# Expert weights of a mixture layer in 1 MB quarters, with the first gate matrix loaded in the stage before

## The reference, cut to what matters

```python
g_idx  = argmax(t @ w_rg + b_rg)                  # one of 4 groups for each token
ids, w = top-2 of the 8 experts of that group     # so 512 (token, expert) pairs over 32 experts
y_e    = (silu(h @ w_gate[e]) * (h @ w_up[e])) @ w_down[e]   # 2048 -> 512 -> 2048
x      = x + gate * sum_e combine[:, e] * y_e
out    = modulated RMS norm of x
```

## Time and profile before

| what | value |
|---|---|
| median of 3 runs | 2301.48 us (2300.1 to 2301.67) |
| the profiled execution's own time | 2300.72 us |
| its span, from first to last instruction | 2299.0 us |
| mean granted TensorE clock | 0.990 |
| TensorE matmul busy | 2142.7 us, 93% |
| VectorE busy | 1379.7 us, 60% |
| ScalarE busy | 731.1 us, 32% |
| moved by DMA | 760.64 MB, mean 331 GB/s |

### The profile page before, as it was taken

One profiled execution on the slowest core, in us unless ns is written; L12 is line 12 of the kernel. 1 busy time (PEld: TensorE's weight loads), 2 busy tenths in 40 slices (PEclk: granted clock), 3 DMA queues, 4 the chain that ended last, 5 costly groups with the idle time before them and its releaser, 6 DMA issues. The chain is left out here.

```text
span 2299.0 us, 35407 instructions
## 1 busy us (share of the span) xinstructions
PE 2142.7 (93%) x14337; PEld 1621.8 (71%) x14337; DVE 1379.7 (60%) x2163; ACT 731.1 (32%) x1324; POOL 40.9 (2%) x62
## 2 busy tenths in 40 slices
PE   7999999999999999899999979998898888898886
PEld 6899999888999998788898755554444444444443
DVE  6888889988888899755556453333333333333334
ACT  6444554554445554556555320000000000000001
POOL 0010000000000000020000000000000000000000
PEclk9999999999999999999999989999999999999998
DMA  8898777988887779654344189999999999999996
GB/s 336 339 341 324 281 266 282 351 341 334 331 326 279 268 278 370 239 207 161 137 147 151 51 355 429 431 430 429 429 432 430 432 430 429 429 432 429 432 428 288
DMA packets 72496, 760.64 MB, mean 331 GB/s; under 512 B 8224, under 2 KB 11200, under 8 KB 13888
## 3 DMA queue, kind: packets, MB, share of 16 engines
q1 hardware_dynamic: 72240, 758.31, 82.3%
q10 hardware_dynamic: 144, 0.79, 0.1%
HBM read 756.12 MB, written 2.95 MB: 330 GB/s over the span
## 5 line engine op out<-in xcount | busy, mean ns | idle before, releaser
L1230 DVE TENSOR_TENSOR s_w_tail<-s_raw,s_w_head 128x1024 fp32r<-128x1024 f32 x292 | 345.7, 1226 | 19.1 <-ACT s_w_head L832 19.0
L1020 PE MATMUL b_ps<-s_h_head,s_w_head 128*128 128x256 f32 x1184 | 340.9, 288 | 0.0
L832 ACT ACTIVATE s_w_head<-s_raw 128x1024 fp32r<-128x1024 f32 x292 | 294.4, 1052 | 141.1 <-DMA s_raw<-in_w 87.7
L1021 PE MATMUL b_ps<-s_h_tail,s_w_head 128*128 128x256 f32 x1184 | 334.8, 283 | 0.0
L1022 PE MATMUL b_ps<-s_h_head,s_w_tail 128*128 128x256 f32 x1184 | 334.8, 283 | 0.0
L1345 DVE CUSTOM_DVE_ANT_0 s_raw<-s_raw,s_c_row 128x2048 f32<-128x2048 f32 x128 | 292.6, 2286 | 0.2
L2464 PE MATMUL b_ps<-s_raw,s_window 128*64 128x256 f32 x2048 | 227.6, 380 | 38.7 <-DMA s_raw<-in_w_up 20.7
L2464 PEld LDWEIGHTS b_ps<-s_raw,s_window 128*64 128x64 f32 x2048 | 155.2, 137 | 116.3 <-issue 30.6
L1020 PEld LDWEIGHTS b_ps<-s_h_head,s_w_head 128*128 128x128 f32 x1184 | 226.7, 192 | 4.2 <-issue 3.9
L1021 PEld LDWEIGHTS b_ps<-s_h_tail,s_w_head 128*128 128x128 f32 x1184 | 227.0, 192 | 0.3
L1022 PEld LDWEIGHTS b_ps<-s_h_head,s_w_tail 128*128 128x128 f32 x1184 | 226.8, 192 | 0.0
(11 more groups left out here) (356 smaller groups left out, 3429.5 us busy)
## 6 DMA issues: line engine op xcount, KB each, us to landing
s_raw<-in_w SPq DMA_DIRECT2D x198, 1024.0 KB, 5.1
s_raw<-in_w_ada SPq DMA_DIRECT2D x128, 1024.0 KB, 6.2
s_raw<-in_w_gate SPq DMA_DIRECT2D x16, 4096.0 KB, 32.8
s_raw<-in_w_up SPq DMA_DIRECT2D x16, 4096.0 KB, 30.7
s_raw<-in_w_down SPq DMA_DIRECT2D x32, 2048.0 KB, 26.9
s_down<-in_w_down SPq DMA_DIRECT2D x16, 2048.0 KB, 27.2
s_spare<-in_w_gate SPq DMA_DIRECT2D x8, 4096.0 KB, 32.9
s_down<-in_w_gate SPq DMA_DIRECT2D x8, 4096.0 KB, 32.9
```

The source lines that it names most:

```text
L832: act.activation(w_head[:, g % SPLITS, cols], raw[:, ring, cols], ACT.Copy)\
L1020: pe.matmul(out, head, m_head, start=first, stop=False, skip_group_check=True)
L1021: pe.matmul(out, head, m_tail, start=False, stop=False, skip_group_check=True)
L1230: dve.tensor_tensor(w_tail[:, g % SPLITS, cols], raw[:, slot["w", g], cols], w_head[:, g % SPLITS, cols].bitcast(F32), ALU.subtract)\
```

## The change

- The ring keeps its four slots of 4 MB, but every matrix is loaded as four quarters of 1 MB (8 KB for a partition out of rows of 32 KB), each with an arrival semaphore of its own (`arrived[slot][q]`) and a release of its own: `used` goes up 12 times for an expert instead of 4, and SP waits for one quarter's release before it loads that quarter.
- Slot 0 (`first_slot`) is allocated ahead of the second attention, whose ka, kb, v, s_buf, p_t, squares and one of the two q buffers now lie in it. SP loads the gate of expert 0 into it at the end of the second attention's list, after the last weight piece and after `onorm B`. `experts` then loads only up and down of expert 0 at its start.
- `x_head` and `x_tail` become one buffer `x_parts`, in four quarters by width, which lie over the four quarters of slot 3; quarter q of expert 1's gate is loaded when 4(q + 1) tiles are gathered.
- `window` is copied in two halves; the first half of the first window is copied in the middle of the gather, and TensorE starts expert 0 with it.
- Semaphores of the first block are used again in the second attention, with counts that run on. The router logits are put in `o_rstd` instead of q.

```diff
+        full(sp, ("onorm", "B"))
+        for q in range(QUARTERS):
+            sp.dma_start(first_slot[:, q, :], d["w_gate"][0, :, q * CHUNK_ELEMS:(q + 1) * CHUNK_ELEMS])\
+              .then_inc(first_arrived[q], 16)
...
-        x_head, x_tail = (passing.enter_context(nc.sbuf_tensor(f"s3_{name}", [P, TT, D], F32R))
-                          for name in ("x_head", "x_tail"))
+        x_parts = passing.enter_context(nc.sbuf_tensor("s3_x_parts", [P, QUARTERS, 2, TT, 512], F32R))
...
+    def load_quarter(sp, e, c, q, slot):
+        src = (w_gate, w_up, w_down)[c][pick_e, :, q * CHUNK_ELEMS:(q + 1) * CHUNK_ELEMS]
+        sp.dma_start(ring[slot][:, q, :], src.rearrange("a p n -> (a p) n")).then_inc(arrived[slot][q], 16)
+    def arrival(eng, seq, q, turns_before=0):
+        eng.wait_ge(arrived[seq % SLOTS_E][q], turns_before * 16 + (seq // SLOTS_E * 16 + 16))
...
-        for c in range(PIECES_E):
-            load_expert_piece(sp, 0, c)
+        for c in (1, 2):
+            for q in range(QUARTERS):
+                load_quarter(sp, 0, c, q, c)
...
-            sp.wait_ge(sem["gathered"], KT)
             for c in range(PIECES_E):
-                if c:
-                    sp.wait_ge(sem["used"], min(c, 2))
-                load_expert_piece(sp, 1, c, 1)
+                for q in range(QUARTERS):
+                    seq = PIECES_E + c
+                    if c == 0:
+                        sp.wait_ge(sem["gathered"], KT // QUARTERS * (q + 1))
+                    else:
+                        sp.wait_ge(sem["used"], QUARTERS * (seq - SLOTS_E) + q + 1)
+                    load_quarter(sp, 1, c, q, seq % SLOTS_E)
...
                     for c in range(8):
-                        if c % 4 == 0:
-                            pe.wait_ge(arrived[(3 * j + c // 4) % 4], ...)
+                        if c in (0, 2):
+                            pe.wait_ge(sem["window"], of(2, 1 + c // 2))
+                        arrival(pe, PIECES_E * j + c // 4, c % 4, four * PIECES_E)
                         ...
-                        if c % 4 == 3:
-                            ins.then_inc(sem["used"], 1)
+                        ins.then_inc(sem["used"], 1)
...
                     for m_ in range(FT):
-                        if m_ == 0: ...
-                        elif m_ == 2: ...
+                        arrival(pe, PIECES_E * j + 2, m_, four * PIECES_E)
                         ...
-                        if m_ % 2:
-                            ins.then_inc(sem["used"], 1)
+                        ins.then_inc(sem["used"], 1)
...
+            if m == 9:
+                dve.wait_ge(sem["read_a"], 4)
+                dve.wait_ge(sem["read_v"], 4)
+                dve.tensor_copy(window[:, 0:8, :], picked[:, 0:8, 0:WINDOW]).then_inc(sem["window"], 1)
...
-        dve.tensor_copy(window[:, :, :], picked[:, :, 0:WINDOW]).then_inc(sem["window"], 1)
+        dve.tensor_copy(window[:, 8:KT, :], picked[:, 8:KT, 0:WINDOW]).then_inc(sem["window"], 1)
```

More of the change, by code:

```diff
@@ L58, with __init__ @@
 class Tally:
-    def __init__(self):
+    def __init__(self, before=None):
         self.order = {}
+        self.before = before or {}
     def add(self, sem, event, it=0):
@@ L67, in add @@
         assert (event, it) not in table, (sem, event, it)
-        table[event, it] = len(table) + 1
+        table[event, it] = self.before.get(sem, 0) + len(table) + 1
     def at(self, sem, event, it=0, each=1):
@@ L1485, in _ @@
             x_done(dve, DEPTH - 1)
+    passed_on = [f"full{b}" for b in range(8)] + [f"raw{n}" for n in range(RAW)]
+    return {name: sem[name] for name in passed_on}, {name: len(tally.order[name]) for name in passed_on}
 HEADS_2 = 16
@@ L2208, with experts @@
 SLOTS = PICKED + WINDOW
[L2209 removed]
+PIECES_E = 3
+USED_E = PIECES_E * QUARTERS
 TAIL_AT = {1: 1, 3: 2, 7: 3}
 PART_BANKS = ((0, 1, 2, 3), (6, 7, 4, 5))
[L2216 removed]
+def experts(nc, whole, ctx, d, x, ssq_x, c0, mod, mod_dram, out, shared, first_slot, arrived):
     sem_names = ["consts", "squared", "rstd", "affine", "read_a", "read_v", "dense_row", "dense_h", "exp_in", "exp", "pairs", "sums", "sums_read", "starts", "x_head", "x_tail", "picks",
                  "gathered", "window", "used", "gate_exp", "hidden", "turned", "hidden_t", "y_half",
[L2230 removed]
+                 "weights_t", "y_scaled", "part", "x_added", "out_ready", "stored", "rows", "dense_gate", "dve_chain", "pool_chain"]
     sem = {n: whole.enter_context(nc.semaphore(f"b3_{n}")) for n in sem_names}
[L2232 to L2233 removed]
     def sb(name, shape, dt=F32):
         return ctx.enter_context(nc.sbuf_tensor(f"s3_{name}", shape, dt))
[L2238 to L2240 removed]
+    second_slot = sb("second_slot", [P, QUARTERS, CHUNK_ELEMS])
+    third_slot = sb("third_slot", [P, QUARTERS, CHUNK_ELEMS])
     picked = sb("picked", [P, KT, SLOTS])
@@ L2343, in _ @@
                     for c in range(PIECES_E):
-                        sp.wait_ge(sem["used"], four * (4 * PIECES_E) + (PIECES_E * (j + 1) + min(c, 2)))
-                        load_expert_piece(sp, four * 4 + (j + 2), c, j + 2)
+                        for q in range(QUARTERS):
+                            seq = PIECES_E * (j + 2) + c
+                            sp.wait_ge(sem["used"], four * (4 * USED_E) + (QUARTERS * (seq - SLOTS_E) + q + 1))
+                            load_quarter(sp, four * 4 + (j + 2), c, q, seq % SLOTS_E)
             for e in (EXPERTS - 2, EXPERTS - 1):
                 for c in range(PIECES_E):
-                    sp.wait_ge(sem["used"], PIECES_E * (e - 1) + min(c, 2))
-                    load_expert_piece(sp, e, c, e)
-            sp.wait_ge(sem["used"], PIECES_E * (EXPERTS - 1))
+                    for q in range(QUARTERS):
+                        seq = PIECES_E * e + c
+                        sp.wait_ge(sem["used"], QUARTERS * (seq - SLOTS_E) + q + 1)
+                        load_quarter(sp, e, c, q, seq % SLOTS_E)
+            sp.wait_ge(sem["used"], USED_E * (EXPERTS - 1))
         for n, row in ((2, mod_dram[7:8, :]), (1, mod_dram[6:7, :])):
@@ L2519, in _ @@
                 for c in range(PIECES_E):
-                    pe.wait_ge(arrived[c] if c < 3 else second_half[0], e * 16 + 16)
+                    for q in range(QUARTERS):
+                        arrival(pe, c, q, e)
                 for side in range(2):
@@ L2684, in _ @@
                 loop.link(dve.tensor_tensor(hid, psum[:, 0, 0:T], hid, ALU.mult))
-                dve.wait_ge(sem["used"], e * PIECES_E + 2)
+                dve.wait_ge(sem["used"], e * USED_E + 2 * QUARTERS)
                 dve.tensor_tensor(hidden[:, 1, :], psum[:, 1, 0:T], hid, ALU.mult).then_inc(sem["hidden"], 1)
                 start = dve.value_load(starts_i[0:1, bass.ds(e + 1, 1)], min_val=0, max_val=PICKED)
-                dve.tensor_copy(window[:, :, :], picked[:, :, bass.ds(start, WINDOW)]).then_inc(sem["window"], 1)
+                for ks in (slice(0, 8), slice(8, KT)):
+                    dve.tensor_copy(window[:, ks, :], picked[:, ks, bass.ds(start, WINDOW)]).then_inc(sem["window"], 1)
                 for b in range(2):
@@ L2810, in build @@
                                       ("gain3", [P, KT]), ("sconst", [P, 36]))}
+        first_slot = ctx.enter_context(nc.sbuf_tensor("first_slot", [P, QUARTERS, CHUNK_ELEMS], F32))
+        arrived = [[ctx.enter_context(nc.semaphore(f"b3_arrived{slot}_{q}")) for q in range(QUARTERS)]
+                   for slot in range(SLOTS_E)]
         with ExitStack() as part:
-            second_attention(nc, ctx, part, d, x, ssq_all, c0, mod, mod_dram, shared)
+            second_attention(nc, ctx, part, d, x, ssq_all, c0, mod, mod_dram, shared, first_slot, arrived[0],
+                             ring_sems, ring_counts)
         with ExitStack() as part:
-            experts(nc, ctx, part, d, x, ssq_x, c0, mod, mod_dram, out, shared)
+            experts(nc, ctx, part, d, x, ssq_x, c0, mod, mod_dram, out, shared, first_slot, arrived)
```

94 lines of the change are left out of this document (42 added, 52 removed).

## The result

The changed kernel took 2309.54 us (median of 5, 2308.65 to 2311.17) against 2301.48 for the kernel before: ratio 1.0037, 95% interval 1.0025 to 1.0049. The forecast was 2308.9 us, slower. The profiled execution was the slowest of the five, 2311.17 us against 2300.72 before. A second set of runs of the same kernel gave 2311.24 us, 1.0042 (1.0028 to 1.0056).

The account below looks back on a forecast made before the run. The prediction took the expert stage's unbroken weight stream as the bound: last landing +11.4 us at 420.5 GB/s, prefetch included, less 4.0 at the end, gave +7.4, so 2308.9 us median; range 2295 to 2317.

Parts of the forecast that it names:

- What bounds: Expert stage: one unbroken stream of weight transfers at 430 GB/s is the bound, not TensorE.
- The prefetch: Start of the expert stage: early gate of expert 0 and early slot 3 quarters save 3 quarters, 7 us of stream.
- The size of a transfer: Expert stream: 8 KB rows in 1 MB transfers run at 420.5 GB/s instead of 430; last landing +11.4 us.
- The second way: Expert stream: rate from 32 and 16 KB rows (432, 426 GB/s); a cost in each row doubles again, giving 414.5.
- The tail: After the last landing: TensorE takes quarters as they land, done 1.77 us (1.9 with a wait) later, not 5.9; −4.0 us.
- The sum: Later last landing plus shorter end: +11.4 − 4.0 = +7.4 us, 2308.1 profiled, 2308.9 median.
- the signs of being wrong: Expert stage: rate 424 or more, DMA share under 0.98 after 1365 us, or TensorE's clock falling for over two short stretches.
- The fresh rate: Rival on the expert stream: 8 KB rows hold 424 to 427 GB/s; 2295.0 us at 427; chance 0.25.
- size costs nothing: Rival on the expert stream: rate stays at 430 GB/s, giving 2288.6 us; chance 0.07.
- the cost is in each row, or each transfer: Rival on the expert stream: 414.5 GB/s, 2322.3 us (417 gives 2316.7); chance 0.12 together with the late-slot rival.
- The start is not what I think: Rival at the stage's start: slot 3 or 0 frees late, stream breaks, 2 to 5 us lost; within a shared 0.12.

Follow-up runs that it names:

- mixed: The changed kernel with only experts 0 to 3 and 31 in quarters and the 27 between in 4 MB matrices; 2295.29 us, 0.9971.
- mixed_32: The changed kernel with only experts 0 to 2, 30 and 31 in quarters, the others in 4 MB matrices; 2292.71 us, 0.9959.
- parts_32: The kernel before the change, each transfer issued as four of every fourth partition, rows kept at 32 and 16 KB; 2303.52 us, 1.0007.
- no_prefetch: The changed kernel with expert 0's gate loaded at the start of the expert stage, not in the second attention; 2318.42 us, 1.0073.
- apart_8k: The changed kernel, each matrix in two 2 MB transfers of alternate quarters (8 KB rows), arrival and release by full matrix; 2320.28 us, 1.0079.
- halves: The changed kernel with 2 MB pieces (16 KB rows) instead of quarters for load, arrival and release; 2298.02 us, 0.9983.
- whole_arrival: The changed kernel, but TensorE waits for all four quarters of a matrix at the first; loads and releases unchanged; 2314.84 us, 1.0058.
- whole: The changed kernel with 4 MB matrices (32 KB rows) instead of quarters for load, arrival and release; 2300.76 us, 0.9995.

## Why the prediction was right, step by step

**What bounds.** Right: the stream. The DMA share is 1.01 from 1363 to 2262 us, and wherever a run changed rows, landings or prefetch, the last landing moved with the stream. In mixed and mixed_32, as in before and parts_32, TensorE then ends the layer on its own work, without a wait for the last matrix.

**The prefetch.** Right. The early quarters went out at 1274.94 (1274.5 forecast); TensorE began expert 0 at 1362.13, 31.1 us after the stage's first issue (31.6 forecast). Undoing the early gate costs 8.5 us of the stage; I had 7 for gate and slot 3 together, against the kernel before, and 9 for this run. What I had not seen is that the gate alone gives this. no_prefetch keeps the early quarters of slot 3 and the early window, and its stage is 965.9 − 949.0 = 16.9 us longer than before; the rate costs 21.3 and the tail gives back 3.9, so these two are worth about 0.5 us, an estimate.

**The size of a transfer.** The term that decided was taken as 420.5 GB/s and measured as 420 to 421. The number was right, and in part by luck. I chose it because the stream would be like the stretch at 903 to 919 us "in size and in depth", and the depth is not the cause: the queue is now 27.3 us deep instead of 8.3 and the rate is the same,

```profile
s_third_slot<-in_w_up SPq DMA_DIRECT2D x32, 1024.0 KB, 27.3
```

The 427 GB/s of the earlier trace rows are not from 8 KB rows alone: from 97 to 107 us, 0.73 of the 4.27 MB went over a second queue.

```profile
q10 hardware_dynamic: 135, 0.73, 17.5%
```

A later stretch is SP's queue alone, with rows of 8 KB, and still over 421; this stays unexplained.

```profile
123.00:132.00 9.00, 9.00 (x64) 8.41 (x63) 6.08 (x7) 4.52 (x6) 0.00 (x0) 1.00 1.01 425
```

The second way, a cost that sits in each row, is the mechanism that parts_32 and apart_8k show. I had it only as a bound and among the rivals, at 414.5 GB/s with a small chance. It was too low, because 426 GB/s, read from 8 us, is 428 in a long stretch (halves). With 428 the same working gives 420.2, which is the measured rate.

In a queued stream no fixed cost of microseconds is paid for each transfer in line: parts_32 has four times the transfers of before at 429 GB/s, and after lands 1 MB every 2.49 us. The Trainium skill gives a fixed cost of about 2.0 us for each transfer ("DMA: Bandwidth & Descriptors", section Anatomy of one DMA — SWDGE (gpsimd) path), measured on transfers issued from GpSimd, while these are issued from SP. The prediction tied this cost to the 341 GB/s of the page's section Bandwidth, which does not state it as their cause; no run here measures a transfer by itself.

**The tail.** Right: 1.94 us behind the last arrival, 1.9 forecast. With whole_arrival, which gives up the arrival by quarters, the stage is 5.4 us longer.

**The sum.** Forecast +7.4 us for the stage, measured 957.7 − 949.0 = +8.7. The tail gave the −4.0 forecast within 0.1 us; the last landing came some 1.2 us later than forecast, 0.8 of them from the first stretch (1365 to 1500 us ran at 418 GB/s, which the sum had at 420.5). In the profiled execution the late start of the stage, 1.7 us, comes on top; the medians differ by 8.1 us. None of the signs of being wrong came: no rate of 424 or more, no share under 0.98, and a clock of 1.00 from 1363 to 2262 us.

**The rivals.** The fresh rate (424 to 427 GB/s) and "size costs nothing" fell with the 421. Of "the cost is in each row, or each transfer", the transfer fell with parts_32; the row was the true mechanism, with too high a price. "The start is not what I think" did not come: the stream was not broken.

## What to carry to other kernels

When a stage is one unbroken stream of transfers, finer pieces buy only what happens before its first byte and after its last; in the middle they cost what each row costs, if they shorten the rows. Cut the transfers where that pays, at both ends, and keep rows long between: here 0.9959 of the time before instead of 1.0037. To cut a transfer without shortening its rows, cut across partitions: four transfers with every fourth partition each ran at 429 GB/s against 430. A block of 32 neighbouring partitions was not tried.

## What the hardware showed beside it

A row of a transfer costs about 11 ns beside its bytes (an estimate from 432, 428 and 421 GB/s with rows of 32, 16 and 8 KB), and it does so with the engines fully busy, at a DMA share of 1.00 to 1.01.

TensorE's granted clock changes with how its waits are spread. With the same rate of 421 GB/s, whole_arrival's stretch shows 0.97 where after's shows 1.00:

```profile
1600.00:2000.00 400.00, 353.70 (x2388) 207.97 (x2386) 134.18 (x176) 16.16 (x39) 0.00 (x0) 0.97 1.01 421
```

Its waits are up to 1.9 us long, after's at most 0.6:

```profile
PE b_ps L2506 <- DMA s_third_slot<-in_w_down: 11.3, 6, 1.9
```

The length alone does not decide, for before has 25 waits of up to 1.9 us and shows 1.00 in the same stretch; parts_32, with 25 of up to 2.0 us at the same place, shows 0.98. These two wait at up, between two long blocks of matmuls. whole_arrival waits at down, just behind the turn of the hidden values, where TensorE does little in any case, and so do whole, mixed and apart_8k, which show 0.97 to 0.98. No run takes the place by itself, so its part is not shown. One wait at down, from the end of up on:

```profile
1623.00:1626.00 3.00, 1.15 (x8) 0.41 (x4) 1.19 (x3) 0.86 (x2) 0.00 (x0) 1.00 1.03 429
1626.00:1630.00 4.00, 3.81 (x10) 1.42 (x12) 0.00 (x0) 0.00 (x0) 0.00 (x0) 0.57 1.01 418
```

Behind such a wait the clock can go to the lower of its two levels (1.2 instead of 2.4 GHz) for a while; it does not do so each time. In mixed, down of expert 30 took 8.78 us after a wait of 1.74, instead of 7.09. The stream takes 29.9 us for an expert and TensorE 27.2, and this slack hides the loss in the middle of the stage. In halves, with waits of about 1 us, the stretch shows 1.00. That arrival by quarters or halves keeps the clock up was not expected. It brought nothing in the middle, since TensorE is not the bound there; near the end, whole and mixed each lost 1.7 us on a matrix by waits of a whole matrix.

Left open: why the granted clock near the start, and with it the beginning of the expert stage, differs from profile to profile, and why 8 KB rows run at 425 GB/s for a few us in the first block.
